# Tiles 2 and 3 of the gated row sum on TensorE, with identity turnings ahead of them

## What is computed

```python
def moe_ffn(x, router_w, router_b, w_gu, b_gu, w_down, b_down):
    ...
    top_logits, top_idx = lax.top_k(logits, TOP_K)
    gates = jax.nn.softmax(top_logits, axis=-1)
    ...
    y_slots = lax.map(run_block, (slot_tok.reshape(n_blocks, MOE_BLOCK), block_expert)).reshape(-1, D)
    slot_of = jnp.zeros((n_assign,), jnp.int32).at[order].set(dest)
    y = jnp.einsum("tk,tkd->td", gates.astype(x.dtype), y_slots[slot_of].reshape(n_tok, TOP_K, D))
    return y.reshape(B_, L, D)

def second_block(...):
    ...
        h = h + moe_ffn(rms_norm(h, norm_ffn_g[l]), router_w[l], ...)
    return rms_norm(h, final_norm_g)
```

## Time and profile before

| | |
|---|---|
| median of 3 runs | 2981.2 us (2977.5 to 2983.76) |
| the profiled execution | 2974.19 us |
| its span | 2972.2 us |
| TensorE busy in the span | 2770.5 us, 93% |
| VectorE busy | 1626.7 us, 55% |
| ScalarE busy | 1053.7 us, 35% |
| mean granted TensorE clock | 0.966 of full |

### The profile page before, as it was taken

One profiled execution on the slowest core, in us unless ns is written; L12 is line 12 of the kernel. 1 busy time (PEld: TensorE's weight loads), 2 busy tenths in 40 slices (PEclk: granted clock), 3 DMA queues, 4 the chain that ended last, 5 costly groups with the idle time before them and its releaser, 6 DMA issues. The chain is left out here.

```text
span 2972.2 us, 35142 instructions
## 1 busy us (share of the span) xinstructions
PE 2770.5 (93%) x13480; PEld 1990.4 (67%) x13524; DVE 1626.7 (55%) x2488; ACT 1053.7 (35%) x1485; POOL 197.7 (7%) x250
## 2 busy tenths in 40 slices
PE   7878999999999999999998889899999999998897
PEld 6656778888887788888877567455556555554352
DVE  4874545444455554434766653676566655564254
ACT  4444444222223442222334223033444433342031
POOL 0530000000000000000001303000000000000002
PEclk9989999999999999999999978899999999999999
DMA  4110324444333132222221005889999999999988
GB/s 137 57 57 1 114 93 156 177 160 164 151 117 113 61 113 97 99 100 85 75 84 57 1 1 188 330 332 411 413 415 414 405 409 410 405 402 408 373 325 328
DMA packets 185692, 612.01 MB, mean 206 GB/s; under 512 B 12451, under 2 KB 18242, under 8 KB 185122
## 3 DMA queue, kind: packets, MB, share of 16 engines
q1 hardware_dynamic: 166992, 552.34, 48.4%
q10 hardware_dynamic: 11282, 39.90, 3.4%
q0 software_dynamic: 7200, 16.79, 1.5%
HBM read 574.39 MB, written 44.04 MB: 208 GB/s over the span
## 5 line engine op out<-in xcount | busy, mean ns | idle before, releaser
L91 DVE TENSOR_TENSOR unit_low<-unit_whole,unit_high 128x4096 fp32r<-128x4096 f32 (+3 forms) x95 | 287.2, 3029 | 173.5 <-ACT unit_high L88 162.6
L674 PE MATMUL psum<-tokens_high,unit_high 128*128 128x512 f32 (+2 forms) x1016 | 372.1, 366 | 3.8 <-PEq L870 1.6
L674 PE MATMUL psum<-tokens_high,unit_low 128*128 128x512 f32 (+2 forms) x1016 | 368.3, 363 | 0.0
L674 PE MATMUL psum<-tokens_low,unit_high 128*128 128x512 f32 (+2 forms) x1016 | 368.2, 362 | 0.0
L88 ACT ACTIVATE unit_high<-unit_whole 128x4096 fp32r<-128x4096 f32 (+2 forms) x65 | 225.8, 3474 | 374.1 <-PE psum L674 287.2
L3758 PE MATMUL psum<-ring_slot,hT 128*64 128x512 f32 x1184 | 270.7, 604 | 13.8 <-DMA ring_slot<-in_moe_w_gu 13.8
L91 DVE TENSOR_TENSOR moe_low<-ring_slot,moe_w_high 128x1024 fp32r<-128x1024 f32 x236 | 275.4, 1219 | 2.9 <-ACT moe_w_high L88 2.7
L88 ACT ACTIVATE moe_w_high<-ring_slot 128x1024 fp32r<-128x1024 f32 x236 | 245.8, 1057 | 50.3 <-PE psum L3943 48.7
L674 PEld LDWEIGHTS psum<-tokens_high,unit_high 128*128 128x128 f32 (+1 forms) x1016 | 190.9, 188 | 37.0 <-issue 3.8
L674 PEld LDWEIGHTS psum<-tokens_low,unit_high 128*128 128x128 f32 (+1 forms) x1016 | 190.9, 188 | 31.7 <-issue 1.6
L674 PEld LDWEIGHTS psum<-tokens_high,unit_low 128*128 128x128 f32 (+1 forms) x1016 | 190.9, 188 | 30.7 <-issue 0.2
(11 more groups left out here) (685 smaller groups left out, 4867.2 us busy)
## 6 DMA issues: line engine op xcount, KB each, us to landing
ring_slot<-in_moe_w_gu SPq DMA_DIRECT2D x112, 2048.0 KB, 24.1
ring_slot<-in_moe_w_down SPq DMA_DIRECT2D x56, 2048.0 KB, 24.4
unit_whole<-in_w_up SPq DMA_DIRECT2D x16, 2048.0 KB, 7.9
unit_whole<-in_w_down SPq DMA_DIRECT2D x16, 2048.0 KB, 7.8
unit_whole<-in_moe_w_gu SPq DMA_DIRECT2D x16, 2048.0 KB, 24.3
expert_rows<-zero_row ACTq DMA_DIRECT2D x15, 1536.0 KB, 5.3
unit_whole<-in_moe_w_down SPq DMA_DIRECT2D x8, 2048.0 KB, 23.4
unit_whole<-in_w_in SPq DMA_DIRECT2D x5, 2048.0 KB, 7.8
```

The costliest lines, as they stand in the source:

```text
L91: return dve.tensor_tensor(self.low, self.whole, self.high.bitcast(F32), ALU.subtract)
L674: ins = pe.matmul(bank, a, c, start=(first and m == 0), stop=(last and m == len(parts) - 1))
```

## The change

Tile 2's rows are summed by TensorE too. VectorE makes eight gate matrices in place of four, in the two halves of a buffer of which one half was used. In `combine`, VectorE leaves out tile 2's four multiply-adds, and tile 2's `add_last` moves from ahead of all scalings to a place behind the scalings of tiles 0 and 1. TensorE makes the `selT` products alone for tiles 0 and 1 only, then 50 transposes of the identity into bank 6, and then the full sums of tiles 2 and 3, each behind a wait for its rows.

```diff
+    ON_VECTOR = 2
...
-        self.gate_tile = T.xg[:, 0].rearrange("p f s -> p (f s)")[:, 0:4 * P].rearrange("p (n s) -> p n s", n=4)
+        self.gate_tile = T.xg[:, 0].rearrange("p (t n) s -> p t n s", n=4)
...
-        for n in range(4):
-            ins = dve.tensor_scalar(self.gate_tile[:, n, :], k.ident[:, :], T.gates[:, TT - 1, n:n + 1], None, ALU.mult)
+        for t in range(self.ON_VECTOR, TT):
+            for n in range(4):
+                ins = dve.tensor_scalar(self.gate_tile[:, t - self.ON_VECTOR, n, :], k.ident[:, :], T.gates[:, t, n:n + 1], None,
+                                        ALU.mult)
         ins.then_inc(self.gates_made.sem, 1)
 
-    def sum_last_tile(self, pe, E):
-
-        k, T, t = self.k, self.T, TT - 1
+    def sum_tile(self, pe, t):
+
+        k, T = self.k, self.T
         pe.wait_ge(self.gates_made.sem, self.gates_made.at(1))
         pe.wait_ge(self.rows_loaded[t], 64)
         for half in range(2):
             bank, cols = k.psum[:, 2 * t + half, :], slice(half * 512, half * 512 + 512)
             pe.matmul(bank, self.late.selT[:, t, :], T.o[:, cols], start=True, stop=False)
             for n in range(4):
-                ins = pe.matmul(bank, self.gate_tile[:, n, :], self.rows(t, n, 1)[:, cols], start=False, stop=(n == 3))
+                ins = pe.matmul(bank, self.gate_tile[:, t - self.ON_VECTOR, n, :], self.rows(t, n, 1)[:, cols], start=False, stop=(n == 3))
         ins.then_inc(self.late.full.sem, 1)
...
         add_last(1)
-        add_rows(2)
-        add_last(2)
         for t in range(TT):
-            if t == TT - 1:
+            if t >= 2:
                 add_last(t)
             self.invert(dve, t)
             self.scale(dve, t, t + 1)
...
-            finish.late.products(pe, 0, E.o_whole, 2 * STEPS, TT - 1)
-            finish.sum_last_tile(pe, E)
+            finish.late.products(pe, 0, E.o_whole, 2 * STEPS, Finish.ON_VECTOR)
+            k.stay_busy(pe, 6, 50)
+            for t in range(Finish.ON_VECTOR, TT):
+                finish.sum_tile(pe, t)
```

## The result

The changed kernel took 2988.97 us (median of 7 runs, 2982.83 to 2994.58) beside 2977.5 us for the kernel before (7 runs, 2974.42 to 2983.76): a ratio of 1.0031, with a 95% interval of 1.0018 to 1.0043. It is slower by 0.31%, some 9 us by the ratio (the two medians lie 11.5 us apart), where 0.7 us more was forecast. The forecast was 2981.9 us in a range of 2977.0 to 2986.5, and the median lies 2.5 us above that range. A second comparison, with 12 runs of the changed kernel and 35 of before, gave 1.0015 (1.0007 to 1.0024), some 4.5 us. In both the changed kernel is slower. The two intervals overlap, and why the sizes differ isn't shown.

A forecast was written before the change was run, and what follows sets the result against it. The prediction took tile 3's sum on TensorE to bound the kernel's end. TensorE's end 0.7 us later (8.55 more, 5.1 and 2.65 back), put on the median, gave 2981.9 us, in a range of 2977.0 to 2986.5.

The forecast's parts named there:

- The views and the bound of before: At the kernel's end tile 3's sum on TensorE, 11.5 us, is the largest piece; VectorE has 2.9 us to spare.
- the clock's 2.65: Tile 3's sum in the kernel before runs partly at the lower clock, costing 2.65 us that a warm TensorE regains.
- Parts 1, 4 and 5: Four more gate matrices on VectorE cost nothing; VectorE has 4 us to spare at tile 3; tail unchanged, 7.4 us.
- Part 2: TensorE's queue ahead of tile 2's sum: 50 turnings end at 2947.7, rows land at 2948.07, clock still high.
- Part 3: The sums of tiles 2 and 3 on TensorE take 17.1 us; its end moves 0.7 us later, to 2965.5.
- 8.55 - 5.1 - 2.65: TensorE's end: 8.55 us more records, less 5.1 us earlier start, less 2.65 us regained clock, giving 0.8 us.
- The range: Bounds on the whole kernel's time, 2977.0 to 2986.5 us, said to leave out about 2 in 10.
- A: Ahead of tile 2's sum the clock falls because transposes don't hold it: 2985.4 us, chance 0.09.
- B: In the last step VectorE was the bound after all: 2975.1 us, chance 0.04.
- C: Code loading puts a 2.5 us gap into TensorE's sums, which costs in full: 2984.4 us, chance 0.07.

The follow-up runs named there:

- before with turnings: The kernel before with 50 turnings added between the selT products and tile 3's sum, tile 2 staying on VectorE: 2983.17 us against 2984.05, ratio 0.9996.
- tile 2 shared: The changed kernel with tile 2's rows 0 and 1 added by VectorE, rows 2 and 3 by TensorE, no turnings: 2981.19 us, 0.9998 of before.
- the kernel before again: The kernel before with no edit, timed against itself and profiled a second time: 2982.65 us against 2981.19, ratio 1.0006.

## Why the prediction was wrong

**The views and the bound of before.** What was read in them stands for that execution. That the sum of tile 3, with its low clock, sets the end showed again in two more profiles of before. That VectorE had time to spare held as well (2.90, 2.89 and 3.11 us in the three profiles of before), but little more than the clock's 2.65: where VectorE starts late and the clock holds, VectorE is the bound (before with turnings). The lower end of the range is called the lowest run of before, which is 2977.5 and not 2977.0; nothing hangs on it.

**Parts 1, 4 and 5** were right in what they conclude. The four more gate matrices cost nothing that shows, VectorE waits some 4 us for tile 3 (4.26 in the profile after), and from the end of the sums to the end of the span it is 7.4 us in every profile in which TensorE is last.

**Part 2 is the step that failed.** It took the start of the `selT` products from one execution, 27.8 us behind the mark, and found that the 50 turnings end 0.4 us before tile 2's landing. It even said that they fill the gap almost exactly. It never asked what happens if TensorE comes later, and there was next to no slack: the products' start plus 8 records and 50 turnings (9.0 us) reaches the landing of tile 2 (37.1) if they start after 28.2. In the three profiles of the changed kernel they start at 35.7, 31.1 and 36.5. From there each us of lateness is paid, since TensorE has 26.3 us to do without a pause: 31.1 + 26.3 = 57.4.

**Part 3's arithmetic was right, its starting point not.** 20 records a tile at 0.43 us gave 8.6 us, and the profile after has 8.6 (2967.6 to 2976.2, and on to 2984.9). But the forecast 8.55 - 5.1 - 2.65 credits an earlier start of 5.1 us, which is there only when TensorE is early. In the changed kernel's own second profile the sums start at 40.1 in place of 42.2 behind the mark: 2.2 us earlier, not 5.1. With that start the same sum, 8.55 - 2.2 - 2.65, gives 3.7 us, which is what this profile has over the first one of before (57.4 against 53.7). In the first they start at 44.7, later than the one sum did before. So the mechanism that the forecast described, work going from the engine that waited to the one that was waited for, was right, and its sign too; its size was wrong by the term for the start. The kernel before hides a late TensorE in its wait for tile 3's rows (42 us behind the mark), and the changed kernel doesn't.

**Why TensorE is late** is shown in part. The down weights of the last expert land anywhere from 17.5 to 21 us behind the mark, while they share the DMA engines with the gathers. A long wait for them lets the clock fall, as in the stretch at 0.50 above, where 16 records took 6.09 us in place of the 3.65 of the earlier trace rows. Where it held and nothing else intervened, the products start 9.9 us behind the landing; where it fell, 11.6 to 12.2. A further pause of up to 6.7 us between TensorE's turning and ScalarE's copy stands in five of the fourteen profiles, two of the three of the changed kernel among them and one of before with 0.6 us; in the other nine the copy starts 0.04 us behind the turning. What makes it is open. The same five profiles, and no others, lack records: 105 to 153 of the landings of their 434 DMAs aren't there, beside 49 in each of the nine, and those of tiles 0 and 1 of the gathers are among them. So the recording itself may make the pause, which isn't shown. It doesn't follow the kernel: all four profiles from one chip have it, each of another kernel, before among them, and none of the eight from another chip, also each of another kernel; for the first two profiles the chip isn't on record. How often it came in the runs that were timed isn't known, and so the gap between the two comparisons, 9 and 4.5 us, stays open.

**The rivals.** A (transposes don't hold the clock) is refuted: 1.00 through all turnings in every profile that has them at this place. The Trainium skill's sentence on it ("TensorE: Matmul & The Clock Gate", Part 4) doesn't hold for these float32 turnings. B (VectorE the bound) is wrong for the changed kernel; VectorE is the bound in the one profile with one tile and a clock that held. C (a pause on TensorE costs in full, being on the path) names the price rightly, and a pause of 2.85 us stood in the profile; but it was placed inside the sums, for code loading, and it came ahead of the products, where the prediction had nothing. The 2.52 us gap of the earlier trace rows, on which C rests, is no code loading: it ends 0.1 us after the down weights land (17.9 us behind the mark, the products at 18.0), so it is the wait for them.

**The range** was built on the scatter of whole runs and on the rivals one at a time. 2986.5 left no room for a late TensorE, because no row had been asked how late it can be.

## What to carry to other kernels

Before work is moved to an engine that waits for a transfer, ask how much of that wait is there in every execution: one profile shows one arrival. Here the point from which the wait is counted moved from 27.8 to 36.5 us in the six profiles of the two kernels, and the wait was a cushion, not free time. Add up the engine's queue from its last release without any wait, and compare that sum with what the other engine has. Work that needs nothing that is waited for (here the `selT` products) belongs ahead of the wait; that, with the tile shared between the engines, gave 0.12%, where moving the whole tile lost 0.15 to 0.31%. A filler has to end before the data lands when the engine comes late, not only when it comes early: 50 more turnings cost 5.8 us, and no filler here gained anything that a comparison shows, though the clock held in the profiles.

## What the runs showed of the hardware

Transposes of the identity at 0.107 us each kept the granted clock at 1.00, and in the 70 turnings of the earlier trace rows it rose from 0.50 to 1.00 with nothing else on TensorE, though they compute nothing that is used. After a pause of 2.91 us the clock stood at 0.50 when work came back; after the pause of 1.45 us that stands ahead of the products in each of these tails it stood at 1.00. The length of a pause alone doesn't tell: after 2.72 us (tile 2 shared) it was 0.50, and after 2.85 us (the kernel before again, ahead of its down products) 1.00 through all 16 records. So the 4 us that the prediction reads between TensorE's last matmul and the fall is that execution's. And with the DMA engines full (a share of 1.02 to 1.03 from 12 to 22 us behind the mark in every profile), the landing of the last 2 MB of weights moved from 17.5 to 20.9 us behind the mark, and three executions of the kernel before were up to 20 us apart at the mark (2911 to 2931) after the same instructions.
